# The low part of the second weight block of the late gate slabs: from VectorE to GpSimd

## The reference, cut to what matters

```
h = h + y
e = rms_norm(p[i] @ ple_proj[i], ple_norm_w[i])
gate = sigmoid(rms_norm(h, ple_gate_norm_w[i]) @ ple_gate_w[i] + ple_gate_b[i])
h = h + gate * e
return rms_norm(h, final_norm_w)
```

## Time and profile before

| | |
|---|---|
| runs of before | 2157.18 us median of 3 (2154.55 to 2157.31) |
| the profiled execution | 2154.96 us, its span 2153.2 us |
| busy | TensorE 2127.8 us, VectorE 1500.1, ScalarE 1020.7, GpSimd 166.3 |
| granted clock of TensorE | 0.993 of full speed, mean |
| low parts of the weights on VectorE (L1794) | 339 instructions, 1220 ns mean |
| high parts on ScalarE (L1267) | 339 instructions, 1048 ns mean |

### The profile page before, as it was taken

How to read it: one execution, slowest core, us unless ns; L and a number is a source line. 1 busy time by engine, 2 the same in 40 slices (tenths; PEclk the granted TensorE clock), 3 DMA queues, 4 the chain that set the end, 5 groups by cost and what they waited for, 6 DMA issues and landing times.

```text
span 2153.2 us, 30167 instructions
## 1 busy us (share of the span) xinstructions
PE 2127.8 (99%) x10138; PEld 1780.9 (83%) x10138; DVE 1500.1 (70%) x2973; ACT 1020.7 (47%) x1914; POOL 166.3 (8%) x244
## 2 busy tenths in 40 slices
PE   9999999999999999999999999999999999999995
PEld 7888888888888888888888888888888888888885
DVE  7577777775676577777676655556667778786887
ACT  7355555553343364444545443345455456433553
POOL 1001111100000000010101010000010000000110
PEclk9999999999999999999999999999999999999997
DMA  9525566655554455353536565344397675898876
GB/s 331 185 100 164 161 173 174 182 164 154 136 167 127 137 148 147 105 177 113 170 111 190 170 176 176 101 134 139 126 330 256 224 266 185 267 263 285 238 198 204
DMA packets 130266, 390.64 MB, mean 181 GB/s; under 512 B 15040, under 2 KB 20544, under 8 KB 128832
## 3 DMA queue, kind: packets, MB, share of 16 engines
q1 hardware_dynamic: 108736, 283.56, 38.8%
q0 software_dynamic: 21440, 105.92, 20.5%
HBM read 339.88 MB, written 139.72 MB: 223 GB/s over the span
## 4 chain that ended last, share of the span: by engine, by line
PE 93%; DVE 4%; issue 1%; DMA 1%; ACT 1%; SPq 0%; ACTq 0%; DVEq 0%; POOLq 0%
PE acc L952 24%; PE acc L954 24%; PE acc L953 24%; PE lv L1044 3%; PE ms L954 2%; PE tr L954 2%; PE tr L953 2%; PE ms L953 2%; PE tr L952 2%; PE ms L952 2%; PE so L1053 1%; PE so L1056 1%; PE so L1033 1%; DVE w_lo L1794 1%; PE tr L1068 1%
## 5 line engine op out<-in xcount | busy, mean ns | idle before, releaser
L952 PE MATMUL acc<-act_hi,w_lo 128*128 128x512 f32 x2384 | 957.7, 402 | 1.6 <-DVE feat L2228 0.5
L954 PE MATMUL acc<-act_hi,w_hi 128*128 128x512 f32 x2384 | 929.4, 390 | 0.0
L953 PE MATMUL acc<-act_lo,w_hi 128*128 128x512 f32 x2384 | 928.5, 389 | 0.0
L1267 ACT CAST w_hi<-w_raw 128x1024 fp32r<-128x1024 f32 x339 | 343.4, 1048 | 440.0 <-PE acc L954 332.0
L954 PEld LDWEIGHTS acc<-act_hi,w_hi 128*128 128x128 f32 x2384 | 447.8, 188 | 94.1
L952 PEld LDWEIGHTS acc<-act_hi,w_lo 128*128 128x128 f32 x2384 | 449.1, 188 | 89.5 <-issue 4.4
L953 PEld LDWEIGHTS acc<-act_lo,w_hi 128*128 128x128 f32 x2384 | 449.3, 188 | 84.1 <-issue 1.1
L1794 DVE TENSOR_TENSOR w_lo<-w_raw,w_hi 128x1024 fp32r<-128x1024 f32 x339 | 402.3, 1220 | 113.9 <-ACT w_hi L1267 108.3
L1343 ACT ACTIVATE work<-work 128x512 f32<-128x512 f32 x120 | 75.3, 628 | 131.4 <-DVE work L1850 130.8
L1864 DVE COPY_PREDICATED work<-mask_sb,lv 128x256 f32<-128x256 uint8 x168 | 88.7, 528 | 7.5
L1281 ACT ACTIVATE work<-work 128x512 f32<-128x512 f32 x64 | 40.5, 632 | 94.1 <-DVE work L1830 94.1
(11 more groups left out here) (372 smaller groups left out, 2505.0 us busy)
## 6 DMA issues: line engine op xcount, KB each, us to landing
w_raw<-in_slabs SPq DMA_DIRECT2D x276, 512.0 KB, 4.4
w_sums<-in_slabs POOLq DMA_DIRECT2D x96, 512.0 KB, 5.6
w_raw<-w_sums SPq DMA_DIRECT2D x64, 512.0 KB, 5.1
w_sums<-w_sums POOLq DMA_DIRECT2D x32, 512.0 KB, 3.9
work<-e_scratch SPq DMA_DIRECT2D x56, 256.0 KB, 4.7
t_sums<-y_scratch POOLq DMA_DIRECT2D x24, 512.0 KB, 6.6
feat<-in_x_feat SPq DMA_DIRECT2D x8, 1024.0 KB, 11.7
e_scratch<-work SPq DMA_DIRECT2D x32, 256.0 KB, 6.3
```

Of the source, the lines that this page charges most:

```text
L952: nc.tensor.matmul(ps, lhs_lo, rhs_hi, start=start, stop=False)
L953: nc.tensor.matmul(ps, lhs_hi, rhs_lo, start=False, stop=False)
L954: return nc.tensor.matmul(ps, lhs_hi, rhs_hi, start=False, stop=stop)
L1267: nc.scalar.copy(w_hi[par][:, j, :], w_raw[j][:, :]).then_inc(w_hi_ready, 1)
```

## The change

From slab 17 on, the low part of block 1 is made by a `tensor_tensor` on GpSimd instead of VectorE: 11 slabs. GpSimd does it for slab n+1 ahead of the accumulating transfer of the first tile of slab n, and behind that of the second tile of slab n-1; slab 27's stands after all transfers. It waits for the high part of the block and for the low part of block 0. VectorE, before it makes the low part of block 0 of the next slab, waits until GpSimd's is counted. Nothing else is changed; the arithmetic is the same.

```diff
+        POOL_LOW = range(17, GATE_SLABS)
...
+            def second_low(n):
+
+                pool.wait_ge(w_hi_ready, (S_GATE + n) * 2 + 2)
+                pool.wait_ge(w_lo_ready, (S_GATE + n) * 2 + 3)
+                g.tensor_tensor(w_lo[n % 2][:, 1, :], w_raw[1][:, :], w_hi[n % 2][:, 1, :].bitcast(F32),
+                                ALU.subtract).then_inc(w_lo_ready, 1)
+
             for q in BY_DMA:
-                h, c = G_TILES[q][0:2]
+                h, c, n, j = G_TILES[q]
+                if j == 0:
+                    second_low(n + 1)
                 pool.wait_ge(*tile_kept(no[h, c]))
                 pool.wait_ge(g2_sum, q + 1)
                 add_to(gate_at(h, c), h_kept[h, c]).then_inc(h_back[q % 4], 16)
+            second_low(GATE_SLABS - 1)
...
             for n in range(GATE_SLABS):
                 before = [G_NO[n - 1, j] for j in range(2)] if (n - 1, 0) in G_NO else []
                 if n + 1 < GATE_SLABS and n:
+                    if n in POOL_LOW:
+                        vec_e.wait_ge(w_lo_ready, (S_GATE + n) * 2 + 4)
                     low_weights(S_GATE + n + 1, (n + 1) % 2, (0,))
                 if before:
                     g_sum_up(before[1])
-                if n + 1 < GATE_SLABS and n:
+                if n + 1 < GATE_SLABS and n and n + 1 not in POOL_LOW:
                     low_weights(S_GATE + n + 1, (n + 1) % 2, (1,))
```

## The result

The changed kernel takes 2167.8 us (median of 5 runs, 2166.24 to 2171.09) against 2154.86 for the kernel before, measured beside it on the same chip (2154.38 to 2157.31). That is 12.9 us slower by the medians; the ratio of the runs is 1.0059, interval [1.0048, 1.007], which makes 12.7. The kernel before came out at 2154.86, where the forecast had started from 2157.18, so the difference missed by more than the time did.

The account below looks back on a forecast made before the run. VectorE's backlog from turn 22 on was taken to set the end. Turns 18 to 21 made it 2.0 us late, turns 22 to 24 gave back 0.8, turn 25 lost 1.0: 2157.18 + 2.2 = 2159.4 us, range 2153.5 to 2166.

Parts of the forecast that it names:

- The sign: Whole kernel: 2.2 us slower forecast; chances faster 0.08, same within 0.2% 0.52, slower 0.40.
- The bound: VectorE's backlog from turn 22 (its pass 22 through the gate-slab loop) to the last slab's result sets the end.
- Removed, 5.6 us: Block 1's subtraction leaves VectorE: 1.14 us a turn, 5.6 us of the chain in turns 22 to 26.
- A lock between the two engines, 4.55 us in turns 22 to 26: GpSimd's subtraction holds VectorE's sigmoid product, 0.7 or 1.05 us a turn; T is the turn's start, block 0's low part.
- Turns 18 to 21: Late reloads and the lock lengthen these VectorE loop passes, so turn 22 starts 2.0 us late.
- The same on GpSimd, 2.08 us: Block 1's 128x1024 subtraction on GpSimd, taken as twice a half-size square of 1.04 us.
- The reload, 5.4 us: SP's next w_raw block 1 load, issued at T + 5.95, lands 5.4 us later, making ScalarE wait in turns under 11.5 us.
- A PSUM operand frees an instruction: VectorE instructions with only one SBUF input are not held; if they were, the sum would be some 2 us later.
- 1: Rival: reload stays slow (6.6 us, giving 2164.4) or GpSimd's subtraction is slower (2.96 us, 4.3 to 10.6 later); chance 0.38.
- 2: Rival: reload in time (5.0 us or less), lock 4.55 against 5.6 saved, 2156.2 us; chance 0.52 together with the forecast.
- 3: Rival: no lock in practice, the chain gets its 5.6 us less 1.2 for the late load, 2152.8 us; chance 0.08.
- 4: Rival: TensorE becomes the bound, block 1 coming later than it wants, 1 to 3 us off the chain; no own chance.

Follow-up runs that it names:

- experiment 6: The changed kernel with GpSimd making block 1's low part for slabs 23 to 27 only: 2161.32 against 2155.45 us for the kernel before.
- experiment 1: The changed kernel, GpSimd only counting where it subtracted, low part of block 1 left out: 2149.76 against 2156.38 us for the kernel before.
- experiment 2: The changed kernel with three GpSimd memsets in the subtraction's place, the low parts left out: 2150.2 against 2156.38 us for the kernel before.
- experiment 7: The changed kernel with a one-column GpSimd memset and a wait between transfer and subtraction: 2156.22 against 2155.45 us for the kernel before.
- experiment 9: The kernel before with six timed GpSimd instructions (memsets, subtractions, a square) at its start: 2159.38 against 2155.79 us.
- experiment 8: The kernel before, VectorE making block 1's low part behind tile 0's logits from turn 16 on: 2153.53 against 2155.45 us.
- experiment 3: The kernel before plus an unused 128x896 GpSimd subtraction at the change's places, all real subtractions on VectorE: 2177.96 against 2156.38 us.

## Why the prediction was wrong

The sign was right and the size was not: +12.9 us for +2.2. The sign deserves little credit: the forecast gave a change too small to measure 0.52. Step by step:

- *The bound.* Right. VectorE's backlog sets the end, TensorE's last wait stays at 9.7 us, and what VectorE loses in turns 22 to 26 goes into the time one to one (6.2 in both traces; experiment 6, which has only this part, is 5.9 slower).
- *Removed, 5.6 us.* Right: turns 22 to 26 are 5.3 and 5.2 us shorter in the traces of experiments 1 and 2, which take it away and put no read in its place. The whole kernels are 6.6 and 6.2 faster, and their intervals (4.7 to 10.8 and 4.1 to 8.2) hold 5.6.
- *A lock between the two engines, 4.55 us in turns 22 to 26.* **This is the step that failed**, in its place and not in its existence. The prediction had GpSimd's subtraction come to the lock at T + 3.3, behind the transfer's issue, wait for the logits and hold the product with the sigmoid for the short rest, 0.7 or 1.05. In the trace the logits, starting at T + 3.18 as forecast and 0.02 ahead of the subtraction's record, are already held: GpSimd has the lock before them, behind an issue that began at T + 2.64 (2097.13 - 2094.49), and VectorE pays nearly the whole length. Instructions of 3.67 (turn 23), 3.26, 3.38 and 2.98 (turns 24 to 26) for 0.69 each lost 3.0, 2.6, 2.7 and 2.3, and one of 1.69 in turn 22 lost 1.0: 11.5 for 4.55. Experiment 7 shows that it was this: with one small instruction and its wait between, GpSimd comes too late for the first one, turns 22 to 26 lose 5.8, and the kernel is 11.9 us below the changed one by the ratios. There the product takes 1.95 in turn 24, 1.26 lost where the prediction had 1.05.
- *Turns 18 to 21.* The prediction had them end 2.0 late, mostly by the reload. They end 9.9 late: 1.7 from the start of turn 17, and 8.2 by the same lock. Each of turns 17 to 21 loses 2.6 to 3.0, 14.7 together, against 5.7 saved, and VectorE's waits for TensorE, 0.70 and 0.55 and one of 0.24 in turn 20, take only 1.5 of that. (The last 0.7 are small waits: the 0.5 of turn 17 and the turns' ends.) This is the larger half of the miss, and it follows from the failed step. That VectorE's lateness would also stop TensorE, 6.5 us for the sum of squares, the prediction did not see; in the changed kernel VectorE waits for TensorE no more in these turns, and it costs nothing there.
- *The same on GpSimd, 2.08 us.* Too small: 2.39 in the kernel and 2.36 in experiment 9 where it runs alone, 2.7 behind a transfer. The square was the wrong neighbour, as it reads one tile twice. The Trainium skill's figure, from which the prediction had estimated 2.25 (GPSIMD Engine Reference, section Performance versus the Vector engine), was nearer, though the runs' 2.36 and 2.39 are above it too.
- *The reload, 5.4 us, which the ledger made cost some 3.* Too dear: block 1's lands in 3.2 to 5.2 us, and no cast waits for it behind turn 17. In part that is luck, as the turns grew to 11.9 us and more by the lock and would have hidden 5.4 too. But experiment 2 had the same late reload with short turns and no lock; there it landed in 3.4 to 3.9 us, ScalarE waited 1.7 in all, and in turns 18 to 26 no low part on VectorE was late for it. Experiment 8 shows the mechanism alive elsewhere, 6.3 us of waits in 8 places. Why the reload is quicker at T + 6 than at T + 3 is not shown.
- *A PSUM operand frees an instruction.* Right: 0.68 in experiment 7 while GpSimd subtracts. The Trainium skill says it of instructions with only one SBUF input (SBUF — State Buffer, Who interferes with whom), and the trace now agrees.
- *The rivals.* 1 was right about a slower GpSimd, and its reload half was wrong. 2 has the reload right and the lock wrong. 3, no lock, fell by the trace and by experiment 3. 4 happened once, late and off the chain: TensorE waits 1.3 us for GpSimd's block 1 of slab 27. Its 4.0 for low parts of block 0 and its 6.5 for the squares come from VectorE's lateness; its last wait is unchanged.

Why the lock goes with the transfer's issue is not shown. That it does is shown by turn 21, where the held instruction starts 0.46 us before the subtraction's record, by turn 24 of experiment 3, where it starts 0.33 before, and by experiment 7. Experiment 7 also moves the subtraction back by 0.5 us (turn 18), and no run delays it without a memset, so whether the delay alone would do is open. Whether GpSimd takes the subtraction in hand during the issue or its record begins late, the traces don't tell apart. One more row bears on it: the one-column memset of experiment 7 takes 0.10 us where no transfer stands just ahead (1991.97) and 0.43 behind one.

## What to carry to other kernels

A GpSimd instruction that reads SBUF can cost VectorE its whole length, so work moved there pays only if VectorE has nothing with two SBUF operands to do meanwhile. GpSimd's memsets held nothing here (experiment 2), and a VectorE instruction with one operand in PSUM was not held (experiment 7). Find the hold in the trace by a VectorE instruction that is longer than its like and ends just behind GpSimd's, and keep a reading instruction from standing right behind a transfer that GpSimd issues; a small memset between was worth 11.9 us. And count what the second engine's lateness does to the third: here it stopped TensorE for 6.5 us. Before handing work to another engine, look for waits inside the busy engine's own order: moving the subtraction, and one scaled tile, into waits of 0.85 and 0.86 us gained 3.8 us where GpSimd lost 12.9.

## What the runs showed of the hardware

- A VectorE instruction that started 0.11 us behind the issue of GpSimd's transfer, and 0.46 before the record of the subtraction behind it, was held. With a memset of 0.43 us between (experiment 7), one that started as early was not.
- A held instruction ends 0.55 us after GpSimd's: 2100.93 for 2100.38 here, as in the earlier trace rows. So the loss is the length of GpSimd's instruction and more.
- A held instruction's wait stands in its own duration and shows as busy time; no view lists it as a wait. VectorE's 15.6 us more of busy time, with 11 instructions fewer, is nearly all such waiting.
- After two waits in the changed kernel TensorE's granted clock fell. Windows of the changed kernel in turn 24 (us, busy of PE, PEld, DVE, ACT and POOL, PEclk, DMA share, GB/s):

```profile
2094.00:2096.00 2.00, 0.14 (x1) 0.17 (x2) 1.73 (x4) 2.00 (x4) 0.00 (x0) 1.00 0.23 40
...
2098.00:2100.00 2.00, 2.00 (x6) 1.52 (x6) 2.00 (x1) 0.00 (x0) 2.00 (x1) 0.50 0.78 109
```

  TensorE stood for 2.3 us up to 2095.86, and from 2098 to 2100 ran at the lower of its levels (0.50 granted, 1.2 GHz), with 6 matmul records for the 10 to 11 of as long a stretch at 1.00. After the 6.5 us up to 2053.66 it was granted 0.50 from 2053 to 2059. After 1.7 us up to 2121.15 the clock stayed at 1.00. Here TensorE has the slack for it; in a kernel that it bounds, a wait for a low part could cost more than its own length, which no run here tries.
